# Three stages of a hybrid layer: runtime loops over token groups replaced by written-out groups

## The chip, the cores and the metric

The kernel runs on one core of one Trainium2 chip. The metric is the device time of one execution in microseconds; lower is faster. The engines are TensorE (PE, with its weight loads as PEld), VectorE (DVE), ScalarE (ACT), GpSimd (POOL) and SyncE (SP, which only issues transfers here). Each runs its own instruction stream, and they meet at semaphores.

## The reference

One residual layer over x of 4096 tokens x 1024, all in float32:

```python
u = rms(x, norm1_g)
q, k, v, x_lru, g_lru = split(u @ w_in)                 # 5 x 512 columns
out_sb  = stick_breaking(q, k, v)                       # 8 heads x 64, causal
xc      = causal_dwconv(x_lru, conv_w, conv_b)          # 4 taps
out_lru = rglru(xc, ...) * gelu(g_lru)                  # h_t = a_t * h_(t-1) + u_t
h = x + concat(rms(out_sb), rms(out_lru)) @ w_out
h = h + hier_moe(rms(h, norm2_g))                       # 4 groups x 8 experts, top 2
y = rms(h, final_g)
```

## The kernel before

The layer is five stages, one after the other, with a barrier of all engines between them. Tokens are handled in NG = 8 groups of GT = 512. Float32 matrices are split into a high and a low part, so each product is three matmuls (high x high, low x high, high x low).

- **Projections** (`qkv`, 0 to about 589 us). For each group, PE forms 12 output tiles of 128 x 512 from 8 chunks of 128 rows (24 matmuls each, L239), transposes the next group's x (L211) and the value differences (L434). ACT and DVE split the results (L484, L525), SP stores them.
- **Recurrence** (`lru`, about 589 to 1006 us). PE forms eight output tiles per group (L380) and the small gate products (L728). ACT, DVE and POOL do the convolution, the gates, the decays and a scan over time (L865).
- **Attention** (`attention`, about 1006 to 2290 us). 8 heads in 4 pairs. The steps of one pair are written out (K/2 = 72 double steps); a runtime loop at L1127 runs that body for the first three pairs, and a written-out copy serves the fourth.
- **Output projection** (`mix`, about 2290 to 2760 us). Per group four tiles of 128 tokens, 48 matmuls each (L1550), the second norm, router logits (L1504), the choice of experts (`select`) and their ranks (`pair_ranks`).
- **Experts** (`experts`, from about 2790 us). A runtime loop of about 80 tiles; it is not touched.

In projections, recurrence and output projection, each engine's program has the first group written out, a runtime loop over the middle groups, and the last group written out (`with engine.Fori(1, NG - 1) as G`). Exceptions: SP's loop of the projections starts at group 0, PE's loop of the recurrence takes two groups a turn (`Fori(1, NG // 2)`), POOL's loop of the recurrence takes all eight groups, and SP's loop of the output projection ends one group earlier. There is no barrier in such a loop: each engine goes round by itself. In the loop, G is a register; a wait such as

```python
dve.wait_ge(qk_high, G * 8 + m + 1)
dve.wait_ge(select_step, h * SELECT_STEPS + count[0] + 1)      # h from G, L1426
```

has its value worked out by register instructions ahead of it, and a transfer's address in DRAM likewise. In a written-out group these are constants. The order of work on each engine is the order of its program; nothing plans it anew.

Of the kernel before, what the change touches and what calls it, by code (L numbers as in the profile page):

```python
# [42 lines left out]
NG = S // GT  # L43
# [49 lines left out]
def hold(engine, k, semaphore, value):  # L93


    engine.wait_ge(semaphore, value)
    engine.sem_inc(k.passed, 1)
# [297 lines left out]
def qkv(nc, k, io, ug, const, next_weights, groups):  # L395

    with ExitStack() as outer:
        sb, ps, sem = alloc(nc, outer)
        weights = SplitWeights(nc, io.w_in[:, 0:3 * W_SB], 3 * W_SB, sb, sem, "qkv_", gain=k.g_norm1)
        with ExitStack() as ctx:  # L400
# [69 lines left out]
            @block.tensor  # L470
            def _(pe):
                hold(pe, k, const.selected, 1)
                hold(pe, k, ug.x_scaled, TT)
                hold(pe, k, ug.lo_ready, 2)
                ug.transpose(pe, 0, 0)
                pe_group(pe, 0, False, NP)
                with pe.Fori(1, NG - 1) as G:
                    pe_group(pe, G, False)
                pe_group(pe, NG - 1, True)

# [31 lines left out]
            @block.scalar  # L512
            def _(act):
                act.wait_ge(const.filled, 1)
                ug.norm(act, 0)
                act.wait_ge(const.gain_loaded, 16)
                first_high(act, weights, ug)
                act_group(act, 0, True, False)
                with act.Fori(1, NG - 1) as G:
                    act_group(act, G, False, False)  # L520
                act_group(act, NG - 1, False, True)

# [24 lines left out]
            @block.vector  # L547
            def _(dve):
                nc.vector.memset(v[:], 0.0).then_inc(v_zeroed, 1)
                dve.wait_ge(v_zeroed, 1)  # L550
                dve.sem_inc(v_carried, NP)
                dve.sem_inc(ug.lo_ready, 2)
                dve.sem_inc(qk_low, 4)
                dve.sem_inc(dv_transposed, NP)
                dve.sem_inc(dv_staged, 2)
                ug.scale(dve, 0)
                first_low(dve, weights, ug)
                dve_group(dve, 0, True, False)
                with dve.Fori(1, NG - 1) as G:
                    dve_group(dve, G, False, False)  # L560
                dve_group(dve, NG - 1, False, True)
                dve.wait_ge(const.selected, 2)
                nc.vector.tensor_copy(k.ident_r[:], k.ident[:]).then_inc(const.filled, 1)
                dve.wait_ge(const.filled, 2)
# [35 lines left out]
            @block.sync  # L600
            def _(sp):
                for s in qk_stored:
                    sp.sem_inc(s, 32)
                for s in dv_stored:
                    sp.sem_inc(s, 16)
                ug.load(sp, 0)
                const.load_gain(sp)
                weights.load(sp)
                const.load_others(sp)
                for c in range(2):  # L610
                    next_weights.load(sp, c)
                with sp.Fori(0, NG - 1) as G:
                    sp_group(sp, G, False)
                sp_group(sp, NG - 1, True)
                sp.wait_ge(const.loaded, 9 * 16)
                sp.wait_ge(u_stored, 32 * NG)
                for s in qk_stored:
                    sp.wait_ge(s, 32 * (2 * NG + 1))
                for s in dv_stored:
                    sp.wait_ge(s, 16 * (2 * NG + 1))  # L620


def lru(nc, k, io, ahead, groups):

    with ExitStack() as outer:
# [6 lines left out]
        with ExitStack() as ctx:  # L632
# [117 lines left out]
            @block.tensor  # L750
            def _(pe):
                pe_group(pe, 0, 0, NL)
                pe_group(pe, 0, 1)
                with pe.Fori(1, NG // 2) as i:
                    pe_group(pe, i, 0)
                    pe_group(pe, i, 1)

# [61 lines left out]
            @block.scalar  # L819
            def _(act):  # L820
                weights.high(act)
                act.wait_ge(step, 2)
                nc.scalar.activation(e[:], relu[:], ACT.Exp, scale=-1.0).then_inc(exp_ready, 1)
                act_group(act, 0, True, False)
                with act.Fori(1, NG - 1) as G:
                    act_group(act, G, False, False)
                act_group(act, NG - 1, False, True)

# [83 lines left out]
            @block.vector  # L912
            def _(dve):
                dve.sem_inc(g_ready, NL)
                dve.sem_inc(out_ready, NL)
                dve.sem_inc(r_ready, 2)
                dve.sem_inc(i_ready, 4)
                dve.sem_inc(th_ready, NL)
                dve.sem_inc(h_ready, NL)
                dve.sem_inc(in_ready, NL)  # L920
                dve.sem_inc(ix_ready, NL)
                weights.low(dve)
                nc.vector.memset(xl[:], 0.0).then_inc(zeroed, 1)
                nc.vector.memset(state[:], 0.0).then_inc(zeroed, 1)
                dve.wait_ge(zeroed, 2)
                dve.sem_inc(x_carried, NL)
                dve.sem_inc(state_ready, NL)
                dve_slope(dve)
                dve_group(dve, 0, True, False)
                with dve.Fori(1, NG - 1) as G:  # L930
                    dve_group(dve, G, False, False)
                dve_group(dve, NG - 1, False, True)
                factors(dve, NG - 1)
                recurrence(dve, NG - 1)

            @block.gpsimd
            def _(pool):
                with pool.Fori(0, NG) as G:
                    for j in range(NL):
                        pool.wait_ge(a_ready, G * NL + j + 1)  # L940
                        pool.wait_ge(stored[j], G * 16 + 16)
                        nc.gpsimd.tensor_tensor(sq[:, j, :], a[:, j, :], a[:, j, :], ALU.mult).then_inc(sq_ready, 1)  # L942
                    for j in range(NL):
                        pool.wait_ge(m_ready, G * NL + j + 1)
                        pool.wait_ge(ix_ready, G * NL + j + NL + 1)
                        nc.gpsimd.tensor_tensor(sq[:, j, :], th[:, j, :], ig[:, j, :], ALU.mult).then_inc(in_ready, 1)
# [352 lines left out]
def mix(nc, k, io, raw_weights):  # L1299


    with ExitStack() as outer:
        sb, ps, sem = alloc(nc, outer)
        weights = SplitWeights(nc, io.w_out, D, sb, sem, "mix_", gain=k.g_mix, ahead=raw_weights)
        with ExitStack() as ctx:
# [58 lines left out]
            def groups(engine, group):  # L1364

                group(engine, 0, True, False)
                with engine.Fori(1, NG - 1) as G:
                    group(engine, G, False, False)
                group(engine, NG - 1, False, True)

# [3 lines left out]
            def load(sp, G, t):  # L1374
                load_mix(sp, k, io, G, t)
                load_x(sp, G, t)
# [11 lines left out]
            @block.sync  # L1388
            def _(sp):
                for s in stored:  # L1390
                    sp.sem_inc(s, 32)
                load_x(sp, 0, 0)
                weights.load(sp, range(weights.depth, weights.depth + 2))
                load_x(sp, 0, 1)
                weights.load(sp, range(weights.depth + 2, DC))
                sp.dma_start(g_norm2[:], io.norm2_g.unsqueeze(0).partition_broadcast(P)).then_inc(params, 16)
                with nc.allow_non_contiguous_dma(reason="router weights, once"):
                    sp.dma_start(w_router[:, :, 0:NGRP], io.w_group.rearrange("(c p) n -> p c n", p=P)).then_inc(params, 16)
                    sp.dma_start(w_router[:, :, NGRP:], io.w_fine.rearrange("(c p) n -> p c n", p=P)).then_inc(params, 16)
                for t in range(2, RING):  # L1400
                    load(sp, 0, t)
                sp.wait_ge(cleared, 1)
                sp.dma_start(io.table.rearrange("(p a n) one -> p a (n one)", p=P, n=P),
                             k.g_dist[:].unsqueeze(1).to_broadcast([P, NE * S // (P * P), P])).then_inc(k.table_cleared, 16)
                sp_group(sp, 0, True, False)
                with sp.Fori(1, NG - 2) as G:
                    sp_group(sp, G, False, False)
                sp_group(sp, NG - 2, False, False)
                sp_group(sp, NG - 1, False, True)

                sp.wait_ge(second_done, 2 * RING + 2 * NT)
                for m, src in enumerate((io.w_e_gate, io.w_e_up)):
                    sp.dma_start(k.ew_raw[:, m, :].rearrange("p (c n) -> p c n", c=DC),
                                 src[0:1].rearrange("e (c p) n -> p (e c) n", p=P)).then_inc(k.ew_loaded[m], 16)
                for s in stored:
                    sp.wait_ge(s, 32 * (NG + 1))
# [986 lines left out]
```

## Time and profile before

| | us |
|---|---|
| median of 3 runs | 4230.46 (4229.04 to 4231.43) |
| the profiled execution, its own time | 4229.56 |
| its span, first to last instruction | 4227.8 |
| PE busy | 4047.8 (96%) |
| DVE busy | 2731.8 (65%) |
| ACT busy | 2429.8 (57%) |
| POOL busy | 790.3 (19%) |

The profile holds one execution. A window is a stretch of it, in microseconds from the span's start. "Busy" leaves out register, branch and semaphore instructions; those are found by source line only, with the engine's name followed by q (PEldq is PE's sequencer). In the table of DMA queues, the kind "instruction" is the fetch of program code itself. An idle time stands with the one whose signal ended it.

### The profile page before, as it was taken

The numbers are of one execution on the slowest core, as the hardware profiler recorded it, in microseconds if no ns is written. First come the engines' busy times: TensorE is split into PE (matmuls) and PEld (weight loads), VectorE is DVE, ScalarE is ACT, GpSimd is POOL, SyncE is SP. The second block draws the span as 40 slices with busy tenths as digits, with TensorE's granted clock in tenths as the row PEclk, the third lists the DMA queues.
The fourth block names the chain that finished last, engine by engine and source line by source line (L and its number), as shares of the span: only waits on it lengthen the run. The fifth ranks groups of instructions, "written<-read, shape, count | busy, mean of one in ns | idle before, by whom it ended". The sixth has DMA issues, their size and how long they took to land. (4 is left out here: it accounts for less than half of the span.)

```text
span 4227.8 us, 87598 instructions
## 1 busy us (share of the span) xinstructions
PE 4047.8 (96%) x29528; PEld 3022.3 (71%) x29529; DVE 2731.8 (65%) x4194; ACT 2429.8 (57%) x3178; POOL 790.3 (19%) x1017
## 2 busy tenths in 40 slices
PE   8999989997999999999998999969999999999997
PEld 6878777775555555555555888848888888888786
DVE  3222226658888888888886666657665655555665
ACT  3222225546887887887885333236665655555665
POOL 0000002222000000000000222224433433333343
PEclk9999999998999999999999999979999999999999
DMA  5444452323011011011102444367666755545674
GB/s 204 174 152 176 149 202 90 119 99 118 22 42 54 30 42 55 28 42 54 35 8 92 157 142 149 120 215 261 240 223 223 244 206 190 204 172 207 241 267 147
DMA packets 315897, 591.10 MB, mean 140 GB/s; under 512 B 44928, under 2 KB 111488, under 8 KB 315664
## 3 DMA queue, kind: packets, MB, share of 16 engines
q1 hardware_dynamic: 264800, 469.80, 31.7%
q0 software_dynamic: 50864, 118.18, 8.1%
q8 instruction: 147, 2.41, 0.2%
q14 instruction: 86, 0.70, 0.1%
HBM read 427.85 MB, written 210.34 MB: 151 GB/s over the span
## 5 line engine op out<-in xcount | busy, mean ns | idle before, releaser
L1153 ACT ACTIVATE att_RT<-att_rt 128x1024 f32<-128x1024 f32 (+1 forms) x576 | 550.6, 956 | 227.0 <-PE att_rt L1091 217.7
L1184 DVE TENSOR_TENSOR_SCAN att_R<-att_stay,att_R 128x257 f32<-128x257 f32 x896 | 625.0, 739 | 26.0 <-ACT att_stay L1143 17.7
L1143 ACT ACTIVATE att_stay<-att_z 128x1024 f32<-128x1024 f32 (+2 forms) x576 | 547.3, 950 | 9.2 <-PE att_z L1077 6.9
L1091 PEld LDWEIGHTS att_rt<-ident,att_R 64*128 64x128 f32 x8448 | 321.5, 139 | 322.3 <-issue 318.6
L1106 PE MATMUL att_out<-att_RT,att_dv 128*64 128x512 f32 (+3 forms) x2304 | 518.0, 570 | 0.0
L1736 DVE TENSOR_TENSOR ew_lo<-ew_raw,ew_hi 128x1024 fp32r<-128x1024 f32 x384 | 443.9, 1217 | 14.2 <-ACT ew_hi L1729 11.8
L1091 PE MATMUL att_rt<-ident,att_R 64*128 64x64 f32 x8448 | 387.4, 228 | 43.3 <-ACT att_RT L1153 32.3
L1729 ACT ACTIVATE ew_hi<-ew_raw 128x1024 fp32r<-128x1024 f32 x384 | 374.1, 1048 | 83.0 <-PE ex_down L2091 76.3
L1187 DVE TENSOR_TENSOR att_R<-att_stay,att_R 128x512 f32<-128x512 f32 x448 | 313.0, 699 | 48.9 <-DVE att_R L1184 2.7
L239 PE MATMUL qkv_out<-u_u_hi,qkv_w_hi 128*128 128x512 f32 x768 | 306.2, 399 | 3.5 <-DVE u_u_lo L230 2.5
L239 PE MATMUL qkv_out<-u_u_lo,qkv_w_hi 128*128 128x512 f32 x768 | 300.0, 391 | 0.0
L239 PE MATMUL qkv_out<-u_u_hi,qkv_w_lo 128*128 128x512 f32 x768 | 299.9, 391 | 0.0
L1106 PEld LDWEIGHTS att_out<-att_RT,att_dv 128*64 128x64 f32 x2304 | 140.1, 136 | 171.3 <-issue 147.2
L1178 DVE TENSOR_TENSOR_SCAN att_R<-att_stay,att_later 128x128 f32<-128x128 f32 (+3 forms) x256 | 195.5, 810 | 69.6 <-ACT att_stay L1143 69.2
L1483 POOL IOTA mix_iota_i<- 128x128 int32 x1 | 0.2, 239 | 1278.2 <-POOLq L85 1278.2
L2135 ACT ACTIVATE ex_h_hi<-ex_h_tr 128x256 fp32r<-128x256 f32 x160 | 52.8, 382 | 323.7 <-PE ex_h_tr L2073 323.7
L525 DVE TENSOR_TENSOR qkv_st_lo<-qkv_out,qkv_st_hi 128x512 fp32r<-128x512 f32 x64 | 44.2, 691 | 282.4 <-ACT qkv_st_hi L484 282.4
L942 POOL TENSOR_TENSOR lru_sq<-lru_a 128x512 f32<-128x512 f32 x32 | 39.8, 1257 | 886.5 <-ACT lru_a L808 886.3
L1550 PE MATMUL mix_out<-mix_w_hi,mix_hi 128*128 128x512 f32 x496 | 201.7, 407 | 0.0
L484 ACT ACTIVATE qkv_st_hi<-qkv_out 128x512 fp32r<-128x512 f32 x64 | 38.3, 598 | 277.6 <-PE qkv_out L239 277.5
L1550 PE MATMUL mix_out<-mix_w_hi,mix_lo 128*128 128x512 f32 x496 | 195.1, 393 | 0.0
L1550 PE MATMUL mix_out<-mix_w_lo,mix_hi 128*128 128x512 f32 x496 | 194.3, 392 | 0.0
(296 smaller groups left out, 8571.8 us busy)
## 6 DMA issues: line engine op xcount, KB each, us to landing
ew_raw<-in_w_e_gate SPq DMA_DIRECT2D x32, 2048.0 KB
ew_raw<-in_w_e_up SPq DMA_DIRECT2D x32, 2048.0 KB
ew_raw<-in_w_e_down SPq DMA_DIRECT2D x32, 2048.0 KB
u_x<-in_x SPq DMA_DIRECT2D x32, 512.0 KB, 6.0
s_u_hi<-u_u_hi SPq DMA_DIRECT2D x8, 2048.0 KB, 11.8
s_u_lo<-u_u_lo SPq DMA_DIRECT2D x8, 2048.0 KB, 16.5
mix_x<-in_x SPq DMA_DIRECT2D x32, 512.0 KB, 4.9
s_h<-mix_h SPq DMA_DIRECT2D x32, 512.0 KB, 3.7
```

The lines of the kernel that those rows point to most:

```text
L239: last = nc.tensor.matmul(bank[:], w[:, c, col:col + P], u[:, c, :], start=(c == 0 and n == 0), stop=(c == DC - 1 and n == 2))
L1091: last = nc.tensor.transpose(rt[:, half, qt, h, :], R[lanes, n % 3, qt, h, s * P:(s + 1) * P], k.ident[lanes, lanes])
L1106: last = nc.tensor.matmul(sums, dv[:, c * TT + s, h * HD:(h + 1) * HD], RT[:, s, first:, h, :, :].rearrange("p t half q -> p t (half q)"), ...
L1143: done = nc.scalar.activation(stay[:, step % 4, :, 0:width], z_pair[:, :, 0:width], ACT.Sigmoid, scale=-scale)
L1153: nc.scalar.activation(RT[:, s, first:, :, :, :].rearrange("p t h half q -> p (t h) half q"), turned_pair, ACT.Copy).then_inc(rt_copied, 1)
L1178: nc.vector.tensor_tensor_scan(R[:, n % 3, s, h, 0:width][:, ::-1], one, later[:, GT - width:][:, ::-1], 1.0, ALU.mult, ALU.max).then_inc( ...
L1184: nc.vector.tensor_tensor_scan(R[:, n % 3, s, h, 0::2][:, ::-1], kept[:, 1::2][:, ::-1], kept[:, 0::2][:, ::-1], R[:, (n - 1) % 3, s, h, 0 ...
L1187: nc.vector.tensor_tensor(R[:, n % 3, s, :, 1:GT:2], stay[:, step % 4, :, 1:GT:2], R[:, n % 3, s, :, 2:GT + 1:2], ALU.mult).then_inc(scann ...
L1550: end = nc.tensor.matmul(half_out[half][n][:], a[:, t, c, :], w[:, c, n * GT:(n + 1) * GT], start=(c == half * NP and m == 0), stop=(c == ...
L1729: self.nc.scalar.activation(self.hi[:, m, cols], self.raw[:, m, cols], ACT.Copy).then_inc(self.high_ready[m], 1)
L1736: engine.tensor_tensor(self.lo[:, m, cols], self.raw[:, m, cols], f32(self.hi[:, m, cols]), ALU.subtract).then_inc(self.low_ready[m], 1)
L2135: nc.scalar.activation(h_hi[:, :, half * HD:(half + 1) * HD], h_tr[half].rearrange("p (f n) -> p f n", f=FC), ACT.Copy).then_inc(h_hi_read ...
```

## The change

Ten runtime loops become Python loops over numbers, so that the body is written into the program once per group: in the projections on PE, ACT, DVE and SP; in the recurrence on PE, ACT, DVE and POOL; in the output projection through the helper `groups` (PE, ACT, DVE, POOL) and on SP. What each group computes, its buffers, its semaphores and the order of instructions stay as they are. Attention's loop and the experts' loops stay runtime loops.

```diff
@@ -474,7 +474,7 @@
                 pe_group(pe, 0, False, NP)
-                with pe.Fori(1, NG - 1) as G:
+                for G in range(1, NG - 1):
                     pe_group(pe, G, False)
                 pe_group(pe, NG - 1, True)
@@ -516,7 +516,7 @@
                 act_group(act, 0, True, False)
-                with act.Fori(1, NG - 1) as G:
+                for G in range(1, NG - 1):
                     act_group(act, G, False, False)
                 act_group(act, NG - 1, False, True)
@@ -556,7 +556,7 @@
                 dve_group(dve, 0, True, False)
-                with dve.Fori(1, NG - 1) as G:
+                for G in range(1, NG - 1):
                     dve_group(dve, G, False, False)
                 dve_group(dve, NG - 1, False, True)
@@ -609,7 +609,7 @@
                     next_weights.load(sp, c)
-                with sp.Fori(0, NG - 1) as G:
+                for G in range(NG - 1):
                     sp_group(sp, G, False)
                 sp_group(sp, NG - 1, True)
@@ -751,7 +751,7 @@
                 pe_group(pe, 0, 1)
-                with pe.Fori(1, NG // 2) as i:
+                for i in range(1, NG // 2):
                     pe_group(pe, i, 0)
                     pe_group(pe, i, 1)
@@ -822,7 +822,7 @@
                 act_group(act, 0, True, False)
-                with act.Fori(1, NG - 1) as G:
+                for G in range(1, NG - 1):
                     act_group(act, G, False, False)
                 act_group(act, NG - 1, False, True)
@@ -927,7 +927,7 @@
                 dve_group(dve, 0, True, False)
-                with dve.Fori(1, NG - 1) as G:
+                for G in range(1, NG - 1):
                     dve_group(dve, G, False, False)
                 dve_group(dve, NG - 1, False, True)
@@ -935,7 +935,7 @@
             def _(pool):
-                with pool.Fori(0, NG) as G:
+                for G in range(NG):
                     for j in range(NL):
                         pool.wait_ge(a_ready, G * NL + j + 1)
@@ -1364,7 +1364,7 @@
                 group(engine, 0, True, False)
-                with engine.Fori(1, NG - 1) as G:
+                for G in range(1, NG - 1):
                     group(engine, G, False, False)
                 group(engine, NG - 1, False, True)
@@ -1403,7 +1403,7 @@
                 sp_group(sp, 0, True, False)
-                with sp.Fori(1, NG - 2) as G:
+                for G in range(1, NG - 2):
                     sp_group(sp, G, False, False)
                 sp_group(sp, NG - 2, False, False)
                 sp_group(sp, NG - 1, False, True)

```

## Rows read from the trace of the kernel before

**Rows 1.** The page: the 40 slices of the span, PE and its granted clock.
```profile
PE   8999989997999999999998999969999999999997
...
PEclk9999999998999999999999999979999999999999
```

**Rows 2.** Windows of loop groups: us, busy (x instructions) of PE, PEld, DVE, ACT, POOL, clock, DMA.
```profile
165.00:235.60 70.60, 70.60 (x386) 56.82 (x385) 17.03 (x33) 18.18 (x34) 0.00 (x0) 1.00 0.45 163
...
793.35:888.80 95.45, 95.45 (x450) 73.83 (x449) 61.93 (x80) 50.42 (x73) 22.41 (x16) 1.00 0.30 110
...
2579.12:2635.68 56.56, 56.56 (x347) 47.19 (x346) 37.45 (x97) 18.48 (x32) 16.49 (x16) 1.00 0.43 148
```

**Rows 3.** The same view, windows of written-out last groups (projections, output projection).
```profile
518.00:588.60 70.60, 69.74 (x368) 55.83 (x366) 13.03 (x27) 12.85 (x23) 0.00 (x0) 1.00 0.46 172
2692.24:2748.80 56.56, 56.56 (x347) 47.19 (x346) 36.90 (x96) 16.54 (x30) 14.96 (x14) 1.00 0.25 94
```

**Rows 4.** Loop control by source line: engine, operation, count: ns min/median/max.
```profile
L477 PEldq FUSED_REGOPS  x6: 50/50/50, 90.9 to 444.2; - x6
L477 PEldq ALU_OP  x6: 32/32/32, 161.4 to 514.4; - x6
L477 PEldq COMPARE_BRANCH  x6: 76/208/243, 161.5 to 514.5; - x6
...
L1367 DVEq COMPARE_BRANCH  x6: 50/56/73, 2413.9 to 2696.6; - x6
```

**Rows 5.** Waits in the projections' loop, 165 to 518 us: us in total, times, longest.
```profile
DVE qkv_st_lo L525 <- ACT qkv_st_hi L484: 182.2, 40, 5.6
ACT qkv_st_hi L484 <- PE qkv_out L239: 179.5, 41, 5.7
```

**Rows 6.** DMA queues: 164:518, 2409:2692, 518:589, 2692:2749 (its q8 row equals 518:589's).
```profile
DMA packets 35360, 57.68 MB, mean 163 GB/s; under 512 B 2080, under 2 KB 12320, under 8 KB 35360
...
q1 hardware_dynamic: 35360, 57.68, 44.5%
...
DMA packets 30720, 41.97 MB, mean 148 GB/s; under 512 B 2560, under 2 KB 23040, under 8 KB 30720
...
q1 hardware_dynamic: 29440, 41.95, 41.9%
q0 software_dynamic: 1280, 0.02, 0.4%
...
q8 instruction: 3, 0.05, 0.3%
q14 instruction: 1, 0.01, 0.0%
...
q14 instruction: 2, 0.02, 0.1%
```

**Rows 7.** The page: instruction queues over the whole span (packets, MB, share of 16 engines).
```profile
q8 instruction: 147, 2.41, 0.2%
q14 instruction: 86, 0.70, 0.1%
```

**Rows 8.** DVE's register work for waits in the output projection's loop.
```profile
L1426 DVEq ALU_OP  x240: 40/40/40, 2371.1 to 2688.1; - x120
...
L1269 DVEq ALU_OP  x96: 40/40/40, 2383.1 to 2696.2; - x96
```

**Rows 9.** Timeline at the recurrence's end, ACT, POOL, DVE, PE: start, us, what, idle before.
```profile
984.62 0.72 ACT L808 ACTIVATE lru_a<-lru_r,lru_slope 128x512 f32<-128x512 f32 x1
...
989.65 1.28 ACT L817 ACT_TABLE_LOAD   x1
990.94 0.63 ACT L817 ACTIVATE lru_th<-lru_th 128x512 f32<-128x512 f32 x1
...
985.58 1.04 POOL L942 TENSOR_TENSOR lru_sq<-lru_a 128x512 f32<-128x512 f32 x1 [17.41 <-ACT lru_a L808]
...
991.73 1.27 POOL L946 TENSOR_TENSOR lru_sq<-lru_th,lru_ig 128x512 f32<-128x512 f32 x1 [1.15 <-ACT lru_th L817]
...
993.04 7.72 DVE L865 TENSOR_TENSOR_SCAN lru_h<-lru_a,lru_state,lru_sq 128x512 f32<-128x512 f32 x4 [1.31 <-POOL lru_sq L946]
...
1008.28 1.65 PE L1077 MATMUL att_z<-chunk 64*128 64x128 f32 x12 [20.05 <-DVEq L1228]
```

**Rows 10.** Attention's untouched loop: its branch by line, then PE's timeline at the first edge.
```profile
L1127 PEldq COMPARE_BRANCH  x3: 79/3400/3401, 1336.1 to 1969.5; - x3
...
1336.42 0.87 PE L1106 MATMUL att_out<-att_RT,att_dv 128*64 128x256 f32 x8
1340.02 0.47 PE L1091 MATMUL att_rt<-ident,att_R 64*128 64x64 f32 x8 [2.73 <-DVE att_R L1187]
```

## The prediction

> **What bounds the kernel now.** I read the page first, then the windows over one group of each touched stage, then the control instructions by line, and last the DMA queues of the same windows. The page's slices put PE at 9 tenths or more nearly everywhere, at a granted clock of 9 tenths or more (of 2.4 GHz), except at the joints between stages [rows 1]. Joints are not what the diff edits, so the windows decide. In each of the three loops PE is busy for all of a group: 70.60 of 70.60 us in the projections, 95.45 of 95.45 us for a pair of groups in the recurrence, 56.56 of 56.56 us in the output projection, at clock 1.00 [rows 2]. "Busy" is modelled for PE, so on its own it does not prove that no time is lost. What proves more is a window of equal length with equal work. DVE needs 17 to 62 us and ACT 18 to 50 us of those windows [rows 2], and in the projections their largest waits run DVE on ACT (182.2 us in 40 waits) and ACT on PE (179.5 us in 41) [rows 5]. PE leads, the others wait for it.
>
> **What goes: the control of the loops.** One turn on PE costs a register operation of 0.050 us, an addition of 0.032 us and the branch, 0.208 us (median) [rows 4]: 0.29 us. PE goes round 6 times in the projections, 3 times in the recurrence (two groups a turn) and 6 times in the output projection, 15 turns: 15 x 0.29 = 4.4 us of sequencer time. On DVE a branch is 0.056 us [rows 4], on ACT, POOL and SP I take no more. Is any of it on the path? The loop of L477 branches from 161.5 to 514.5 us [rows 4], the second time inside the first window of [rows 2], in which the array is never idle: the sequencer issues ahead of the array and has work queued. So the cost is hidden by matmuls that are already queued. The bounds are 0 and -4.4 us; I take 0, because the nearest rows are two whole groups of equal work. In the output projection the loop group of 2579.12 and the written-out last group of 2692.24 both fill 56.56 us with the same 347 matmuls and the same 47.19 us of weight loads, the one with a branch and register values in it and the other with neither [rows 2, 3]. That pair is the experiment, already run inside the kernel before: the group with constants is not shorter by 0.01 us.
>
> **What goes: register work for waits and addresses.** It is largest on DVE in the output projection, where every link of `select` and `pair_ranks` waits for a value made from G: 240 additions at L1426 and 96 at L1269, 0.040 us each [rows 8], so 9.6 + 3.8 = 13.4 us over the whole loop. The cover is DVE's own slack, 56.56 - 37.45 = 19.1 us a group [rows 2]; 13.4 / 6 = 2.2 us a group lies well inside. In the written-out last group DVE's busy time is 36.90 us [rows 3] and PE's rate the same, so I take 0; the bounds are 0 and -13.4 us. SP's address work stands beside transfers whose data is needed a group later. I price it at 0 too: in these windows PE never stands idle for a transfer. If the cover were gone, for instance with a DVE that took 57 us a group, each removed 0.04 us would count in full.
>
> **What is left over: the recurrence's tail.** Here PE has no work, and the engines hand over to each other one by one. Attention's first matmul comes at 1008.28 us after 20.05 us of idle [rows 9]. ACT and DVE have their last group written out already; only POOL's last turn is still a loop turn. Its first square starts at 985.58 us, ACT's decay ended at 984.62 + 0.72 = 985.34: 0.24 us. Its first product starts at 991.73 us, ACT's root ended at 990.94 + 0.63 = 991.57: 0.16 us. A hand-over without register work is that from POOL to DVE, 991.73 + 1.27 = 993.00 to 993.04: 0.04 us. So the first link can shrink by 0.20 us and the second by 0.12 us. The first does not count: ACT's roots start at 990.94 us behind a table load that began at 989.65 us and waits for nothing of POOL's. The second does, because the first scan starts on it and the four scans (7.72 us) then run on one engine. The term is -0.1 us, the bounds 0 and -0.4 us. What is late next is DVE's chain of scans.
>
> **What is added: code that must be fetched.** A loop runs from code that is on the chip: from 164 to 518 us all 35360 packets are data of q1, and from 2409 to 2692 us the 30720 packets are 29440 of q1 and 1280 of q0; no instruction packet in either [rows 6]. Written out, PE's code streams: the last group of the projections fetched 3 packets on q8 and 1 on q14, that of the output projection 3 and 2 [rows 6]. Added are 5 copies of each of these bodies and 2 of the recurrence's pair, for which I estimate 4 packets by its 450 matmuls against 347 to 368: 5 x 3 + 2 x 4 + 5 x 3 = 38 packets on q8, and by the same rows some 5 x 1 + 5 x 1 + 5 x 2 = 20 on q14. The change adds no wait and moves no instruction past another. One packet on q8 lasts 0.2% x 16 x 4227.8 / 147 = 0.92 us [rows 7] (0.7 to 1.2 with the rounding of 0.2%). All 38 on the path would be 35 us. The evidence for 0 is again [rows 3]: three packets came in each of two written-out groups and PE lost nothing in the one with equal work. In the other, PE was busy until it had no more to do, under a DMA share of 0.46, as heavy as in the loop (0.45). I take 0; the bounds are 0 and +35 us.
>
> The Trainium skill, in "Runtime: NRT & Kernel Launch", section "Instruction fetch mechanics", agrees on the cost of streaming and speaks for the change on branches: sequential code is prefetched, but "Branching breaks sequential prefetch", a taken branch to code that is no longer held stalls for a fetch, and kernels are said to prefer full unrolling. This trace shows both halves. By the rule's last clause the change should gain; by its condition (target not held) it should gain nothing here, and [rows 6] show the condition unmet.
>
> **The sum.** 0 (control) + 0 (register work) - 0.1 (tail) + 0 (fetch) = -0.1 us. The profiled execution took 4229.56 us (span 4227.8 us and 1.8 us around it), so the same execution would take 4229.4 us. It lies 0.9 us below the median of 4230.46 us. Against the median I forecast 4230.3 us.
>
> **Rivals.**
>
> (A) *The edges stall, and the change removes the stalls.* Attention's loop shows what an edge costs if the code must come back: PE's branch takes 3.40 us, and the array stands idle for 2.73 us [rows 10]. At the 5 + 2 + 5 = 12 taken edges that PE loses, this would be 12 x 2.73 = 33 us, giving 4197.7 us. Against it: a branch at L477 takes 0.208 us, not 3.4 [rows 4], and no instruction packets flow in those loops [rows 6]. The clause of the skill's page named above would lead here if read without its condition. Chance 0.01.
>
> (B) *The register work is on the path,* of DVE in the output projection and of PE at its turns: 13.4 + 4.4 = 18 us, giving 4212.7 us. For it: PE and DVE do exchange data four times a group in that stage. Against it: the equal windows [rows 2, 3]. Chance 0.03.
>
> (C) *Streaming stalls the array (slower).* The place is each new block of code on PE; the price 0.92 us for a packet that is asked for only when it is needed: 38 x 0.92 = +35 us, giving 4265.4 us. It decides from the point where 9 or more of the 38 blocks are late (9 x 0.92 = 8.3 us). For it: the projections' transfers fill 0.45 of the DMA engines [rows 2], and code waits behind data. Against it: two last groups already stream under that load without loss [rows 3, 6]. Chance 0.04.
>
> (D) *Only the layout moves.* Attention's two taken edges stall now for 2.73 us each; where the target lies in its block of code changes with the code ahead of it. The stall can go (-5.5 us) or a second fetch of 0.92 us and its delay can follow, which I bound by a doubling (+5.5 us): 4224.8 to 4235.8 us. Nothing in the rows says which; the branch cost 3.40 us at both edges, so it repeats. Likewise the moment at which the clock falls at a joint may shift, by a few us. Chance 0.12; about 0.02 of it reaches past 0.2%, half on each side.
>
> **How the numbers follow.** The forecast as worked out has 0.80. 0.2% of the median is 8.5 us, which is also about what a measurement can tell from no change. Within 0.2% lie the forecast and most of (D): 0.90. Faster by more: (A), (B) and a part of (D), 0.01 + 0.03 + 0.01 = 0.05. Slower by more: (C) and a part of (D), 0.04 + 0.01 = 0.05. The range of 8 in 10 goes over the whole of (D) and leaves out (A), (B) and (C): 4224 to 4237 us, the last us for the spread of the runs (2.4 us).
>
> **What would show it.** Right: the windows of 70.60, 95.45 and 56.56 us a group reappear to 0.1 us with PE full; no control instruction at L477, L754 or L1367; in a middle group 3 instruction packets on q8; over the span q8 at about 185 packets in place of 147; POOL's product in the tail starts about 0.05 us behind ACT's root. Wrong: a window that is shorter says (A) or (B); idle time of PE, some us after one another at an even distance of about 20 us, says (C); equal windows but attention longer or shorter by 2 to 6 us says (D). The forecast fails as a whole if the three touched stages together move by more than 2 us.

## The result, and the profile after

| | before | changed | ratio (95% interval) |
|---|---|---|---|
| median, us | 4231.43 (9 runs) | 4241.69 (9 runs) | 1.0021 (1.0012 to 1.0030) |
| profiled execution's span, us | 4227.8 | 4236.4 | |

The change makes the kernel slower by 0.2%: 10.3 us between the medians, 9 us by the ratio, 8.6 us between the two profiled executions. The forecast was no change (4230.3 us) in a range of 4224 to 4237 us; the result lies above it.

I read the page first, then a group of each touched stage. The page of the changed kernel (instruction queues: packets, MB, share):

```profile
q8 instruction: 185, 3.03, 0.3%
q14 instruction: 103, 0.84, 0.1%
```

The code is streamed as forecast: 185 packets where 147 were [rows 7]. Windows of the changed kernel, columns as in [rows 2]: one group of the projections, a pair of groups of the recurrence, a middle and the last group of the output projection.

```profile
449.40:520.20 70.80, 70.80 (x386) 56.83 (x384) 16.96 (x33) 18.18 (x34) 0.00 (x0) 1.00 0.46 163
793.30:888.75 95.45, 95.45 (x450) 73.87 (x449) 61.21 (x80) 50.38 (x73) 23.08 (x16) 1.00 0.31 111
2642.16:2698.72 56.56, 56.56 (x347) 47.21 (x346) 40.86 (x97) 18.50 (x32) 17.60 (x16) 1.00 0.44 149
2698.72:2755.28 56.56, 56.56 (x347) 47.20 (x346) 38.55 (x96) 16.60 (x30) 15.57 (x14) 1.00 0.25 94
```

The groups of two of the three stages run as before [rows 2]. A group of the projections holds the same 386 matmuls in 70.80 us, not 70.60. Over six middle groups that is 1.2 us. Most of the loss is elsewhere, and the first and last start of one line show where. Attention's L1106, before and then changed:

```profile
L1106 PE MATMUL att_out<-att_RT,att_dv x2304: 272/592/1113, 1025.7 to 2282.7; 128*64 128x512 f32 x160, 128*64 128x128 f32 x20, 128*64 128x384 f32 x12
```
```profile
L1106 PE MATMUL att_out<-att_RT,att_dv x2304: 272/593/1113, 1025.1 to 2289.6; 128*64 128x512 f32 x160, 128*64 128x128 f32 x20, 128*64 128x384 f32 x12
```

Attention, which the diff does not touch, went from 1257.0 to 1264.5 us: +7.5 of the +8.6 us. To see where, I time the same matmuls of this line in both kernels: from the 545th to the 641st, which spans the first taken edge of its loop, from the 1137th to the 1233rd, which spans the second, and from the 2241st to the last. Before, then changed (us; PE's busy time and count for this line alone; granted clock; DMA):

```profile
1324.03:1379.07 55.04, 20.68 (x96) 1.00 0.21 66
1648.94:1704.88 55.94, 20.69 (x96) 0.97 0.17 56
2255.05:2282.68 27.63, 13.68 (x63) 0.94 0.05 20
```
```profile
1323.63:1383.28 59.65, 21.98 (x96) 0.94 0.20 61
1653.17:1713.40 60.23, 21.76 (x96) 0.94 0.17 53
2263.49:2289.55 26.06, 12.44 (x62) 1.00 0.06 22
```

The two edges cost 4.6 and 4.3 us more, 8.9 us together, and the stretches before, between and behind them are equal to 0.2 us. The last steps took 1.6 us less, because the kernel before has a short spell at the lower clock there and the changed one has none. PE's timeline of the changed kernel at both edges:

```profile
1336.01 0.87 PE L1106 MATMUL att_out<-att_RT,att_dv 128*64 128x256 f32 x8
1339.87 0.34 PE L1091 MATMUL att_rt<-ident,att_R 64*128 64x64 f32 x4 [2.98 <-DVE att_R L1187]
1342.55 0.48 PE L1091 MATMUL att_rt<-ident,att_R 64*128 64x64 f32 x4 [2.34 <-issue]
...
1661.17 0.34 PE L1091 MATMUL att_rt<-ident,att_R 64*128 64x64 f32 x4 [2.95 <-DVE att_R L1187]
1663.84 0.48 PE L1091 MATMUL att_rt<-ident,att_R 64*128 64x64 f32 x4 [2.33 <-issue]
```

Compare [rows 10]: there PE idles once, 2.73 us, and then does eight transposes in one piece. Here it idles 2.98 us, does four, and idles again for 2.34 us with "issue" as the releaser: it waits for no semaphore. The four transposes that are missing follow directly in the loop's program, with no wait between. What is missing is the code: two packets of q8 start 3.3 us apart at this edge, at 1336.73 and 1340.06 us, and PE goes on 1.3 us after the second has landed. The kernel before fetches two packets as well, at 1337.11 and 1340.42 us, but there PE still has instructions to run while the second comes.

What the second stand (the second idle stretch) sets off is in the windows right behind the first edge, before and then changed (us, busy and count of PE, PEld, DVE, ACT, POOL, granted clock, DMA):

```profile
1341.00:1349.00 8.00, 7.46 (x94) 5.13 (x93) 5.49 (x9) 6.72 (x9) 0.00 (x0) 1.00 0.01 2
```
```profile
1341.00:1349.00 8.00, 6.46 (x34) 3.52 (x35) 4.29 (x7) 2.92 (x4) 0.00 (x0) 0.57 0.02 4
1662.00:1669.00 7.00, 5.16 (x26) 3.17 (x27) 3.23 (x6) 2.92 (x4) 0.00 (x0) 0.54 0.02 5
```

34 matmuls in 8 us where there were 94, at a granted clock of 0.57 of 2.4 GHz, which is the lower level (1.2 GHz) for most of the window; the same at the second edge. And ACT's waits from 1330 to 1345 us, before and then changed (us in total, times, longest):

```profile
ACT att_RT L1153 <- PE att_rt L1091: 4.9, 4, 2.3
```
```profile
ACT att_RT L1153 <- PE att_rt L1091: 6.8, 3, 5.3
```

The second stand costs the array 2.34 us, and attention 4.3 to 4.6 us an edge. At the first edge the clock is at the lower level for 6.8 us and for none before; at the second for 6.8 us where it was for 3.4.

### The profile page after: what moved, and what is told of

The parts are those of the page before. It is cut to its first block and busy times, and to the rows that moved or that the text cites. A ratio compares the mean times of both kernels' runs of the same rounds, so it can differ in the third digit from the quotient of the medians.

```text
span 4236.4 us, 85568 instructions
## 1 busy us (share of the span) xinstructions
PE 4050.6 (96%) x29528; PEld 3023.6 (71%) x29529; DVE 2750.9 (65%) x4194; ACT 2429.1 (57%) x3178; POOL 813.1 (19%) x1017
## 3 DMA queue, kind: packets, MB, share of 16 engines
q8 instruction: 185, 3.03, 0.3%
## 5 line engine op out<-in xcount | busy, mean ns | idle before, releaser
L1106 PE MATMUL att_out<-att_RT,att_dv 128*64 128x512 f32 (+3 forms) x2304 | 519.2, 572 | 0.0
L1106 PEld LDWEIGHTS att_out<-att_RT,att_dv 128*64 128x64 f32 x2304 | 140.5, 136 | 171.9 <-issue 146.5
L1550 PE MATMUL mix_out<-mix_w_hi,mix_hi 128*128 128x512 f32 x496 | 201.5, 406 | 0.0
L1550 PE MATMUL mix_out<-mix_w_hi,mix_lo 128*128 128x512 f32 x496 | 194.9, 393 | 0.0
L1550 PE MATMUL mix_out<-mix_w_lo,mix_hi 128*128 128x512 f32 x496 | 194.3, 392 | 0.0
```

The costliest lines, as they stand in the source:

```text
L1106: last = nc.tensor.matmul(sums, dv[:, c * TT + s, h * HD:(h + 1) * HD], RT[:, s, first:, h, :, :].rearrange("p t half q -> p t (half q)"), ...
L1550: end = nc.tensor.matmul(half_out[half][n][:], a[:, t, c, :], w[:, c, n * GT:(n + 1) * GT], start=(c == half * NP and m == 0), stop=(c == ...
```

## The experiments

All ratios are against runs of the kernel before on the same chip; its medians there were 4231.4 us (changed), 4229.7 (e1 to e4), 4229.3 (e5 to e8) and 4228.7 (e9 to e11). "Attention" is the first to last start of its L1106 (the line moves by up to 6 where a pad was added ahead), from one profile each. The expectations count from attention's first matmul instead, some 17 to 19 us earlier: 1274.4 us in the kernel before, 1282.5 in the changed one, 1264.5 in e3, 1269.5 in e5. A pad is an idle increment of a semaphore, which computes nothing.

| kernel | ratio (95% interval) | median, us | attention, us |
|---|---|---|---|
| before | 1 | | 1257.0 |
| changed | 1.0021 (1.0012 to 1.0030) | 4241.69 | 1264.5 |
| e1 changed, 20 pads on PE | 1.0004 (0.9995 to 1.0013) | 4231.42 | 1257.1 |
| e2 before, 99 pads on PE | 1.0018 (1.0009 to 1.0027) | 4237.35 | 1264.8 |
| e8 before, 56 pads on PE | 1.0006 (0.9997 to 1.0015) | 4232.00 | 1257.9 |
| e3 before, attention written out | 0.9974 (0.9965 to 0.9984) | 4219.23 | 1247.3 |
| e4 changed, attention written out | 0.9981 (0.9972 to 0.9990) | 4221.84 | 1250.3 |
| e5 projections and attention | 0.9992 (0.9983 to 1.0001) | 4225.33 | 1251.1 |
| e6 recurrence, output, attention | 0.9978 (0.9969 to 0.9987) | 4220.87 | 1248.7 |
| e7 as e4, one wait less | 0.9981 (0.9971 to 0.9990) | 4222.74 | 1250.0 |
| e9 as e5, 20 pads on ACT | 0.9989 (0.9980 to 0.9998) | 4224.11 | 1250.0 |
| e10 as e5, 173 pads on PE | 0.9994 (0.9985 to 1.0003) | 4226.53 | 1252.5 |
| e11 as e5, both pads | 0.9987 (0.9978 to 0.9996) | 4223.60 | 1250.2 |

Attention taken apart, by the same matmuls as above (us):

| kernel | first edge | second edge | last steps |
|---|---|---|---|
| before | 55.0 | 55.9 | 27.6 |
| changed | 59.7 | 60.2 | 26.1 |
| e1 | 55.4 | 57.8 | 26.1 |
| e2 | 58.8 | 59.4 | 26.1 |
| e8 | 55.3 | 56.4 | 26.1 |
| e3 | 52.4 | 53.1 | 26.0 |
| e4 | 52.3 | 53.3 | 27.6 |

**e1 and e2: move the code, change nothing else.** At the end of PE's program of the recurrence:

```diff
+                for _pad in range(20):        # e1; 99 in e2, on the kernel before
+                    pe.sem_inc(k.passed, 1)
```

> The changed kernel with 20 idle semaphore increments added on PE at the end of the recurrence, where PE waits for DVE anyway (13 us or more of idle), and nothing else. In the trace of the changed kernel PE comes back from attention's first edge, issues about 14 instructions and then stands for 2.6 us while a second packet of code is fetched; 20 more instructions ahead push the loop's target over the boundary of that block. Theory L (layout: the target lies within the last few instructions of a block of PE's code, so each of the two taken edges pays for two fetches in a row): the second stand goes at both edges, attention falls from 1282.5 us to about 1275 us and the kernel to about +1 us against the kernel before (4232 to 4234). Rival S (the written-out code itself makes attention slow, by its size or its state at attention's entry): still +8 to +10 us (4240 to 4242).

> The kernel before, all loops kept, with 99 idle semaphore increments on PE at the end of the recurrence: the loop target of attention then lies at the same place in its block of code as in the changed kernel (197 against 98 of 256 in the compiled program). Theory L: attention gets both second stands, about +4 us at each edge, kernel +7 to +9 us (4238 to 4241), with nothing of the change in it. Rival S: the same as before, within 1 us, as PE is idle where the increments run.

Both came out by attention's time (1275.0 us in e1 as the expectation counts it) and by the timelines; e1's median is 0.6 us and e2's 0.7 us below what was expected. PE's timeline at the first edge, e1 (two lines later in the source):

```profile
1341.82 0.47 PE L1093 MATMUL att_rt<-ident,att_R 64*128 64x64 f32 x8 [2.71 <-DVE att_R L1189]
```

and e2:

```profile
1340.69 0.47 PE L1093 MATMUL att_rt<-ident,att_R 64*128 64x64 f32 x8 [2.65 <-DVE att_R L1189]
1340.93 0.72 PE L1079 MATMUL att_z<-att_k_hi,chunk 64*128 64x512 f32 x3
1343.59 0.58 PE L1079 MATMUL att_z<-att_k_hi,chunk 64*128 64x512 f32 x1 [1.94 <-issue]
```

With 20 instructions more the changed kernel has one idle stretch per edge again. With 99 more, the kernel before, all loops kept, has two, and its attention is as slow as the changed one's (edges +3.8 and +3.4 us). Instructions that compute nothing cost attention what the whole diff costs it, so the written-out groups are not the cause there. That e1's attention is equal to the kernel before's to 0.1 us is partly luck: its second edge takes 1.9 us more, with PE's clock at 0.51 from 1658 to 1665 us though there is no second stand, and its last steps take 1.6 us less.

**e8: how much code is enough.** The same edit with 56.

> The kernel before, all loops kept, with 56 idle increments on PE at the recurrence's end: by the place of the second stand in the changed kernel (after about 14 instructions, target at 197 of 256 in the compiled program) the loop's target, here at 154, has 57 instructions to its block's end; the kernel before has 113 and shows no second stand, 14 cost 2.0 to 2.6 us at each edge. Theory L in its finer form (the second fetch runs from PE's coming back, about 3 us, and only what the sequencer can issue before it lands is free): a part of the second stand, 0.5 to 2 us at each edge, kernel +1 to +5 us. If a whole block is waited for whatever is left in it, no stand, like the kernel before.

The finer form missed: there is no second stand at either edge. The traces say how much code each build still had when it stood. In the changed kernel PE runs 14 instructions of the loop and stands for 2.3 us; in e2 it runs about 29 (eight transposes and three of the four `att_z` matmuls of the rows above are among them) and stands for 1.9 us. e8 has 43 instructions fewer ahead of the loop than e2, so its block has between 57 (counted from the changed kernel) and 72 (from e2) left. That the two builds stand some 15 instructions apart, though the place of the loop in the program differs by none, I can't explain. Nor do the places in the compiled program fit as they are: a target at 197 of 256 would have 59 instructions left, and the traces show 14 and 29. That the place decides is shown by e1 and e2; where exactly a block ends is not. Between 29 and 57 nothing was tried. (e8's median is 4232.00 us; its attention differs from the kernel before's by 0.9 us.)

**e3 and e4: no edge at all.**

```diff
-            with engine.Fori(0, NP - 1) as hp:
+            for hp in range(NP - 1):
```

> The kernel before with attention's loop over the first three head pairs written out on PE, ACT and DVE; the loops of the change stay. Theory L: no edge, no stand: the 2.73 us at each of two edges go, with what follows them, so -5 to -7 us (4224 to 4227). Rival C (streamed code stalls): every pass already streams, so no loss either; a rise would speak for stalls from size alone.

> The changed kernel with attention's loop written out as well. Theory L: no edge is left for the layout to act on, so the kernel falls by 13 to 16 us against the changed one (to 4226 to 4229), and the distance to the kernel before with attention written out is the change's own price without the layout: about +1 to +2 us, from 0.2 us a group in the projections. Rival S: it stays 7 us or more above that kernel.

Both fell further than expected (4219.23 us for 4224 to 4227, 4221.84 for 4226 to 4229). In e3 attention takes 1247.3 us against 1257.0, but the edges are only a part of these 9.7 us: they gave 2.7 and 2.9 us, 5.5 together, which is the 2 x 2.73 us of array idle and no more. The last steps gave 1.6 us, and 2.6 us lie in small differences elsewhere. e3 is the best version of the study, 10.5 us below the kernel before. The distance between e4 and e3 is 2.6 us by the medians. It is not the change's own price alone: attention differs by 3.0 us between the two, 1.6 of it in the last steps.

**e5, e6, e7: which part carries that price.** e5 writes out only the projections' loops (the first four hunks of the diff), e6 only the others, both on e3. e7 is e4 with

```diff
-            pe.wait_ge(weights.low_ready, c + 1)
+            if G == 0:
+                pe.wait_ge(weights.low_ready, c + 1)
```

> Attention written out in all four passes (so that no edge of its is left), and of the change only the projections' loops written out. The trace of the changed kernel shows a group of the projections at 70.79 us against 70.60 in the loop, all of it in three places at the group's head, where PE's array waits for the low part of u: 0.306 us from matmul to matmul against 0.25. Theory W (the written-out form costs 0.2 us a group there): +1.0 to +1.3 us against the kernel before with attention written out (0.9974 of the kernel before), so 0.9976 to 0.9978. Rival R (the rest of the change carries it): 0.9974, no group of the projections longer than 70.60 us.

> The complement: attention written out, the projections' loops kept, the recurrence's and the output projection's written out. Theory W: nothing, 0.9974 within 1 us, a pair of groups of the recurrence at 95.45 us and a group of the output projection at 56.56 us as in the loops. Rival R: +1 to +2 us here.

> The changed kernel with attention written out, and PE's wait for the projection weights' low part (which all groups repeat ahead of each leading product) kept in group 0 alone; later groups need it no more, since PE has passed it. In the written-out groups of the changed kernel two constant waits meet ahead of one matmul, and the one for u's low part, which comes last, stands on a semaphore instruction of PE's sequencer, the satisfied one on the weight load; in the loop it is the other way round, because register arithmetic carries the satisfied one. Theory W2 (that placing costs the 0.055 us at each of three places a group): the group returns to 70.60 us, -1.0 to -1.3 us against the changed kernel with attention written out (0.9981). Rival F (fetching code costs the 0.2 us): 70.79 us a group as before.

That the repeated wait carries the 0.2 us a group is settled by e7's windows of two middle groups of the projections, written out and yet as short as the loop's:

```profile
378.60:449.20 70.60, 70.60 (x386) 56.79 (x385) 16.96 (x33) 18.16 (x33) 0.00 (x0) 1.00 0.46 164
449.20:519.80 70.60, 70.60 (x386) 56.77 (x385) 16.97 (x33) 18.16 (x33) 0.00 (x0) 1.00 0.46 164
```

Code fetch is the same in e7 as in e4 (178 packets on q8 against 179), so it costs nothing there. Where the wait sat can be read by line. PE's sequencer at L237, before and then changed:

```profile
L237 PEldq EVENT_SEMAPHORE  x141: 51/51/1118, 18.8 to 578.1; - x141
L237 PEldq ALU_OP  x24: 32/32/42, 91.2 to 455.2; - x24
```
```profile
L237 PEldq EVENT_SEMAPHORE  x165: 51/51/1118, 19.0 to 580.0; - x165
```

The 24 additions that carried the old, satisfied wait are gone, and 24 semaphore instructions of 0.051 us stand in their place. At three places at a group's head the wait for the late low part of u was on the weight load in the loop; in the written-out form it is on the semaphore instruction ahead of it, and the matmul behind the waiting one starts about 0.30 us after it instead of 0.25. e7 takes away the instruction and the changed order together, so which of the two costs the time is not shown. The whole-kernel time of e7 does not show the 1.2 us (0.9981 like e4): the projections' first group took between 74.6 and 77.5 us in these profiles, 74.6 in e4's and 77.4 in e7's. e6 came out at +1.6 us for an expected 0, within its interval. e5 missed: +6 us against e3 by the medians (+7.6 by the ratios) where 1.0 to 1.3 were expected. Its groups took the expected 0.2 us more each, 1.2 us in all, and attention took 3.8 us more; the remainder can't be placed: in the two profiles the stages' first groups took 5.2 us more and the experts 4.4 us less, and over all thirteen profiles the first groups vary by 3 to 4 us each and the experts by 7, without an order by kernel.

**e9, e10, e11: why attention differs though its code is the same.**

> What is open: with attention written out, its time still differs between kernels whose attention code is the same: 1264.5 us (all touched loops kept) against 1269.5 us (projections written out), in slips of 0.28 us at even distances of some 70 to 140 us. This kernel is the latter (projections and attention written out) with 20 idle increments on ACT at the recurrence's end, which puts ACT's attention code at the same place in its blocks as in the faster one (42 of 128 in the compiled program, before 22). Theory A (the slips come where ACT's code crosses from block to block): attention back to 1264 to 1266 us, kernel -4 us (0.998). Rival P (PE's blocks): no change, 1269 us, 0.999. Rival N (neither, a state of the run): no change here nor in the next two.

> The same kernel with 173 idle increments on PE, 73 ahead of its first matmul and 100 at the recurrence's end, where it is idle: PE's attention code stands at the same place in its blocks as in the faster kernel (214 of 256 in place of 41). Rival P: attention back to 1264 to 1266 us. Theory A: 1269 us as before.

> Both pads together. Theory A or P: attention at 1264 to 1266 us, like the one of the two that has its own cause. Rival D (DVE's blocks, which stand at 92 against 60 of 128 and aren't moved here): the slips stay in all three, 1269 us. Rival N: 1269 us too, or a value apart from the other two without an order.

By the totals theory A missed: counted as the expectations do, attention took 1268.3 us in e9 and 1268.5 in e11, where it wanted 1264 to 1266, against 1269.5 in e5 and 1270.8 in e10. By the single slips ACT's place decides where they come, and PE's does not. Lining up L1106's matmuls with e3's, e5 and e10 slip by 0.28 us at the same 14 places, e9 and e11 at the same 4 other places. One such place in ACT's timeline of e5, between two steps without it:

```profile
1120.41 1.03 ACT L1153 ACTIVATE att_RT<-att_rt 128x1024 f32<-128x1024 f32 x1 [0.60 <-PE att_rt L1091]
...
1125.21 1.03 ACT L1153 ACTIVATE att_RT<-att_rt 128x1024 f32<-128x1024 f32 x1 [0.88 <-PE att_rt L1091]
...
1129.73 1.03 ACT L1153 ACTIVATE att_RT<-att_rt 128x1024 f32<-128x1024 f32 x1 [0.60 <-PE att_rt L1091]
```

ACT stands for 0.88 us instead of 0.60: the slip of 0.28. Ten slips fewer are worth 2.8 us, and attention came down by only 1.1 us (e9 against e5) and 2.3 us (e11 against e10), not by the 3.5 to 5.5 of theory A. Its size missed for two reasons: 4 slips remain, and e4, e7, e9 and e11, like the kernel before, lose 1.6 to 1.7 us in attention's last few steps at the lower clock, which the changed kernel, e1, e2, e3, e5, e6, e8 and e10 do not. e11's larger gain is e10's loss: e10 lost 1.1 us more than e5 in attention's first steps. The line's longest matmul tells the two kinds apart, in e3 and then e9 (ns min/median/max, first and last start; L1108 is e9's L1106):

```profile
L1106 PE MATMUL att_out<-att_RT,att_dv x2304: 272/592/644, 1023.7 to 2271.0; 128*64 128x512 f32 x160, 128*64 128x128 f32 x20, 128*64 128x384 f32 x12
```
```profile
L1108 PE MATMUL att_out<-att_RT,att_dv x2304: 272/592/1112, 1027.4 to 2277.4; 128*64 128x512 f32 x160, 128*64 128x128 f32 x20, 128*64 128x384 f32 x12
```

What makes the clock fall there in one kernel and not in the other stays open. The traces say more of the slips than their spacing. The packets of q14, the other engines' queue, are of 8 KB (103 packets, 0.84 MB), half of PE's on q8, so I take them as 128 instructions where PE's have 256. Counted through e5's trace, all 14 slips stand at the same remainder, 13, of ACT's instructions divided by 128, and e9's 4 at 17; the same count for DVE and PE gives a different remainder at nearly every slip. So they come with ACT's passage from one block of code to the next. Why only 14 and 4 of some 18 such passages slip is open, and the stall itself was not seen.

## Why the prediction was wrong

- **Control and register work at 0: right.** The recurrence's and the output projection's windows are unchanged to 0.01 us with all loop control gone, and DVE's 13.4 us bought nothing. Rivals (A) and (B) are out.
- **Register work in the projections at 0: wrong by +1.2 us.** I gave a loss no bound there and used the pair of equal windows from the output projection for all three stages. The projections' own pair [rows 2, 3] was unequal in work (386 and 368), and I passed over it. The mechanism is a repeated wait that, once its value was a constant, became an instruction of its own and changed places with the wait for late data, which the step "what goes" did not consider: removing arithmetic can lengthen a path. e7, without the repeated wait, is back at 70.60 us a group.
- **The tail at -0.1 us: right.** The changed kernel's timeline there, ACT and then POOL:

```profile
990.33 2.19 ACT L817 ACTIVATE lru_th<-lru_th 128x512 f32<-128x512 f32 x4
...
991.04 6.76 POOL L946 TENSOR_TENSOR lru_sq<-lru_th,lru_ig 128x512 f32<-128x512 f32 x4 [1.05 <-ACT lru_th L817]
```

  ACT's first root lasts 0.63 us as in [rows 9], to 990.96, and POOL's product starts 0.08 us later, in place of 0.16.
- **Streaming at 0: right in the touched stages**, with 185 packets on q8 as forecast. Rival (C) is out: e7's streaming groups lose nothing.
- **Attention's untouched loop: the step that failed.** The sum has no term for it; the layout stood at 0 there and only as rival (D), and (D) was the case. It had the place (attention's two edges), the cause (what lies ahead of a loop moves its target in a block) and a second fetch. Its chance was 0.12 and its price +5.5 us by "a doubling" of 2.73 us. Measured: +8.9 us at the two edges, 4.3 to 4.6 an edge, and -1.6 us in the last steps (a shift of the clock, which (D) had named without a price): 7.5 us. The fetch was not the error: a second stand of 2.34 us is less than the doubling allowed. The size failed because I priced the idle of the array and not what it sets off: the granted clock fell to its lower level (1.2 GHz) for 6.8 us behind each second stand, and ACT's wait for PE grew from 2.3 to 5.3 us. e1's second edge has the slow clock without the second stand: 3.4 us more of it than before cost 1.9 us. A stand that brings little or no slow clock costs about its idle time: e3 got back 5.5 us for two stands of 2.73.
- **The range** therefore ended too low. With 8.9 us for (D) in place of 5.5, and 1.2 us for the projections, it would have gone to about 4240 us. The median is at 4241.7, beside a kernel before at 4231.4 in the same comparison, 1 us above the three runs that the forecast started from.

The Trainium skill, "Runtime: NRT & Kernel Launch", section "Instruction fetch mechanics", says that code comes in blocks of 16 KiB, 256 instructions, and that a taken branch whose target is outside the held window stalls for a fetch of the target's page. The runs agree: 185 packets for 3.03 MB are 16 KB each, and attention's branch takes 3.40 us where the others take 0.21. The page names a stall for this one fetch only; read that way, the change, which leaves attention's edges alone, would cost them nothing. e1 and e2 show that here the place of the target decides whether one fetch is waited for or two.

The recurrence took 2.5 us less in the changed kernel's profile, in its first 144 matmuls. Twelve other profiles of it lie between 390.0 and 392.9 us (first to last matmul) without an order by kernel, and the changed one at 389.3, so I give it no cause. The experts, which the diff does not touch, took 2.4 us more (from L1550's last matmul to the end); I give that no cause either.

## What to carry to other kernels

A runtime loop can pay at each taken edge because its code has to come back: here attention's, with about 7600 instructions of PE a turn, does, and those of 720 to 940 do not. Look in the trace for a branch of 3 us instead of 0.2 us, and write that loop out, not the small ones whose edges are hidden. Any edit ahead of such a loop, even one that only adds instructions, can move its time by several us: before a difference of 0.2% is put down to an edit, pad the program and see whether the difference moves. Compare stretch by stretch between the same instructions, too: a total can be equal because a loss and a gain cancel, as in e1. A window of equal work proves nothing for the next stage; each stage needs its own pair.

## What the hardware showed that I had not expected

- Twenty idle instructions on an idle engine took 7.4 us off attention (6.7 of it at the edges), and 99 put 7.8 us on it (7.2).
- In the output projection DVE is busy for 40.86 us a group in the changed kernel against 37.45 [rows 2], and POOL 17.60 against 16.49, with the same instructions. Both engines are busy at once for 15.3 us of such a group instead of 10.9; that this is why each takes longer was not tested. PE hid it all.
- After a taken edge of attention two code fetches followed each other only 3.3 us apart, in both kernels; a block with 14 or 29 instructions left does not cover that, one with 57 or more does.
